# One encoder layer on one core: products with V all in every second step, a copy on ScalarE, expert ordering in pieces, sixteen unread products

## The reference

```
u = rmsnorm(x); z = u @ w_in      # q-latent, kv-latent, rotary key, two LRU branches
att = softmax((qn @ kn + qp @ kp) * scale) @ v      # 8 heads, 128 queries at a time
lru = bidirectional RG-LRU * gelu(gate)
x = x + concat(rmsnorm(att), rmsnorm(lru)) @ w_out
t = rmsnorm(x)
g = argmax(t @ w_group + b)                          # one of 4 groups
top 2 of the 8 experts of group g, softmax weights * group weight
for e in 32 experts:
    out += gate[:, e] * ((silu(t @ w_gate[e]) * (t @ w_up[e])) @ w_down[e])
y = rmsnorm(x + out)
```

## Time and profile before

| | us |
|---|---|
| median of 3 runs | 710.38 (709.85 to 711.94) |
| profiled execution | 709.74 |
| span of its profile, first to last instruction | 707.9 |
| busy in it: PE / DVE / ACT / POOL | 663.6 / 390.4 / 259.1 / 235.2 |
| moved by DMA | 155.85 MB, 220 GB/s mean |
| mean granted TensorE clock | 0.978 of full |

### The profile page before, as it was taken

The page is one execution under the profiler, slowest core; times in us unless marked ns, Lnnn a source line. Parts: engine busy times, 40 slices in busy tenths (PEclk is TensorE's granted clock), DMA queues, the critical chain, the costliest instruction groups (busy, mean ns, idle before and its releaser), DMA issues.

```text
span 707.9 us, 12135 instructions
## 1 busy us (share of the span) xinstructions
PE 663.6 (94%) x4288; PEld 443.9 (63%) x4288; DVE 390.4 (55%) x914; ACT 259.1 (37%) x482; POOL 235.2 (33%) x295
## 2 busy tenths in 40 slices
PE   3899999999999999999998659999999999999984
PEld 3887887886546666588887645566555555555531
DVE  3673589553975666637888686852323233232327
ACT  5624787733666767722111201111111111111123
POOL 5244254101925559920000131245232322323110
PEclk9999999999999999999999569999999999999999
DMA  7912210020061000063422899999999999999767
GB/s 230 260 46 52 60 33 28 20 107 31 0 234 64 1 2 2 2 237 122 147 90 76 340 384 416 418 413 409 417 415 415 416 416 416 416 415 416 291 250 301
DMA packets 50914, 155.85 MB, mean 220 GB/s; under 512 B 9509, under 2 KB 22949, under 8 KB 42673
## 3 DMA queue, kind: packets, MB, share of 16 engines
q1 hardware_dynamic: 42704, 136.32, 49.8%
q0 software_dynamic: 6432, 12.60, 4.7%
q10 hardware_dynamic: 1728, 6.29, 2.4%
HBM read 169.86 MB, written 19.92 MB: 268 GB/s over the span
## 4 chain that ended last, share of the span: by engine, by line
PE 85%; DVE 7%; DMA 3%; issue 1%; ACT 1%; POOL 1%; SPq 0%; POOLq 0%; DVEq 0%; ACTq 0%
PE bank L1031 17%; PE bank L768 16%; PE bank L1058 10%; PE bank L949 9%; PE bank L806 6%; PE bank L1005 3%; PE bank L789 3%; PE bank L838 3%; PE bank L815 3%; PE bank L723 2%; PE bank L901 2%; PE bank L1044 2%; PE bank L793 1%; PE bank L797 1%; PE bank L830 1%
## 5 line engine op out<-in xcount | busy, mean ns | idle before, releaser
L1031 PE MATMUL bank<-ring,tmp 128*64 128x256 f32 x896 | 100.6, 383 | 3.7 <-issue 3.6
L647 POOL DMA_INDIRECT expert_rows<-mix,row_now x40 | 40.0, 1000 | 161.8 <-ACT mix L1331 146.8
L1031 PEld LDWEIGHTS bank<-ring,tmp 128*64 128x64 f32 x896 | 65.5, 139 | 40.8 <-issue 11.6
L768 PE MATMUL bank<-u_high,w_high 128*128 128x256 f32 (+3 forms) x224 | 77.9, 348 | 4.3 <-DVE u_low L1585 3.0
L768 PE MATMUL bank<-u_high,w_low 128*128 128x256 f32 (+3 forms) x224 | 76.0, 339 | 0.0
L768 PE MATMUL bank<-u_low,w_high 128*128 128x256 f32 (+3 forms) x224 | 75.9, 339 | 0.0
L1324 ACT ACTIVATE rope<-bank 64x256 f32<-64x256 f32 x40 | 15.1, 378 | 144.3 <-PE bank L1031 132.2
L949 PE MATMUL bank<-ring_parts,mix_parts 128*128 128x512 f32 x240 | 64.8, 397 | 0.0
L637 POOL DMA_INDIRECT tmp<-xn_rows,idx_now x22 | 23.1, 1049 | 115.2 <-DMA xn_rows<-tmp 97.9
L1860 DVE SCALAR_TENSOR_TENSOR rope<-rope,bank 64x256 f32<-64x256 f32 x40 | 16.6, 415 | 79.2 <-ACT rope L1324 78.4
L1331 ACT ACTIVATE mix<-bank,gate_now 128x512 f32<-128x512 f32 x40 | 27.5, 687 | 88.0 <-PE bank L1058 88.0
(11 more groups left out here) (317 smaller groups left out, 1222.6 us busy)
## 6 DMA issues: line engine op xcount, KB each, us to landing
ring<-in_w_up SPq DMA_DIRECT2D x28, 1024.0 KB
ring<-in_w_down SPq DMA_DIRECT2D x28, 1024.0 KB
ring<-in_w_gate SPq DMA_DIRECT2D x28, 1024.0 KB
mix<-in_w_gate SPq DMA_DIRECT2D x12, 1024.0 KB, 10.8
mix<-in_w_up SPq DMA_DIRECT2D x12, 1024.0 KB, 13.9
mix<-in_w_down SPq DMA_DIRECT2D x12, 1024.0 KB, 15.1
ring<-in_w_in SPq DMA_DIRECT2D x13, 512.0 KB, 4.2
ring<-expert_rows SPq DMA_DIRECT2D x12, 512.0 KB, 8.5
```

The lines of the kernel that those rows point to most:

```text
L647: po.indirect_dma_start(ys_d.rearrange("r (t n) -> (r t) n", t=2), bass.IndirectOffsetOnAxis(row_now[:, 2 * j + q:2 * j + q + 1], 0), ysb[ ...
L768: last = pe.matmul(psum[u % ZB][0:m, 0:tn], w[:, t % W_RING, k, 0:m], x[:, k, t0:t0 + tn], start=(k == 0 and p == 0), stop=(k == DC - 1 an ...
L1031: last = pe.matmul(psum[q][t * WB:(t + 1) * WB, 0:F], xT[:, j, c, q * WB:(q + 1) * WB], w[:, (t * DC + c) * F:(t * DC + c + 1) * F], start ...
```

## The change

Four edits.

1. **V products.** `values(m, part)` becomes `values(m)`: all products of a pair stand in the even step, none in the odd one. The waits for the copied probabilities (`pTe`) and, for pair 1, for the branch sums (`lrs`) now stand ahead of the `rb` products instead of between them and the V products.
2. **First copies on ScalarE.** The two copies of the first experts' transposed rows go from VectorE (`rows_out(0, 0, 0)` and `(0, 0, 1)`, behind `pack_near`) to ScalarE, which is waiting there.
3. **Expert ordering in pieces.** `order_far` is cut in two (`order_far`, 13 small operations, and `order_steps`, 3 large ones), and these, the 20 `put_expert` calls and `codes_in` are put between the steps of the first four pairs' `pair_silu`, instead of ahead of and between whole pairs. `expert_codes` on TensorE goes from pair 2 to pair 3.
4. **Unread products in the gap.** `idle_work(n)` issues n products of the identity with 384 columns into a bank that nobody reads; 3, 3, 4 and 6 of them are put into the gap. Two waits for `tt` are added ahead of the first two, so that the bank is free. On GpSimd the wait for `idx` goes behind five others.

```diff
-            po.wait_ge(g("idx"), 2)
             po.wait_ge(g("xnst0"), 8 * NT)
...
             po.wait_ge(g("x2st1"), 8 * NT)
+            po.wait_ge(g("idx"), 2)
...
-            def values(m, part):
+            def values(m):
...
+                pe.wait_ge(g("pTe"), 2 * m + 2)
+                for t in range(2):
...
+                last.then_inc(g("rb"), 1)
+                for b in range(blocks):
...
-                if n >= 2:
-                    values((n - 2) // 2, n % 2)
+                if n >= 2 and n % 2 == 0:
+                    values((n - 2) // 2)
...
+            def idle_work(n):
+
+                for _ in range(n):
+                    pe.matmul(psum[7][:, 0:3 * P], ident, consts[:, CONSTS["ident"]:CONSTS["ident"] + 3 * P],
+                              start=True, stop=True)
+            pe.wait_ge(g("tt"), 2 * NT - 2)
+            idle_work(3)
             turn_rows2(NT - 1)
             router(NT - 1)
+            pe.wait_ge(g("tt"), 2 * NT)
             pe.wait_ge(g("x2"), 2 * NT)
             rows_near(0, 2 * NT - 2)
+            idle_work(3)
             ranks(NT - 1)
             rows_near(2 * NT - 2, 2 * NT)
             totals()
+            idle_work(4)
             pe.wait_ge(g("spread"), 1)
...
+            idle_work(6)
             pe.wait_ge(g("xg0"), 16)
...
-            pair_products(0, 2, expert_codes)
-            pair_products(1, 0)
+            pair_products(0, 2)
+            pair_products(1, 0, expert_codes)
...
+            for half in range(2):
+                ac.wait_ge(g("xgp"), half + 3)
+                ac.activation(xT[:, 0, 4 * half:4 * half + 4, :], psum[2 + half][:, :].rearrange("p (c n) -> p c n", c=4),
+                              ACT.Copy).then_inc(g("xT"), 1)
...
             pack_near(v, link)
-            rows_out(0, 0, 0)
-            rows_out(0, 0, 1)
             spread_rows_in(v, link, 0)
-            order_far(v, link)
...
-            pair_silu(0, 0)
+            pair_silu(0, 0, lambda: order_far(v, link))
+            order_steps(v, link)
             tables_out(v, link, 0)
...
+            put_far(0, 5)
+            pair_silu(0, 1, lambda: put_far(5, 9))
+            put_far(9, 12)
+            gates_out(v, 0)
+            put_far(12, 16)
+            pair_silu(0, 2, lambda: put_far(16, NFAR))
             far_firsts(v, link)
             jobs_in(v, link)
-            gates_out(v, 0)
-            pair_silu(0, 2, lambda: codes_in(v, link))
             rounds_in(v, link)
             spread_rows_in(v, link, 1)
-            pair_silu(1, 0)
+            pair_silu(1, 0, lambda: codes_in(v, link))
```

39 lines of the change are left out of this document (16 added, 23 removed).

## The result

The changed kernel takes **707.69 us** (median of 10 runs, 706.24 to 709.59) against 710.65 for the kernel before (10 runs, 709.68 to 714.18): a ratio of 0.9954, with a 95% interval of 0.9941 to 0.9967. The profiled execution took 707.46, with a span of 705.6; the one of before took 709.74. The forecast was 707.0, with 704.0 to 710.0 as its range. Several of its markers were wrong all the same.

The account below looks back on a forecast made before the run. TensorE bounds the kernel ahead of the weight stream; at the last pair weights and TensorE arrive together. 709.74 - 3.2 (attention) - 0 (the rest) = 706.5, given as a median of 707.0, range 704.0 to 710.0.

Parts of the forecast that it names:

- Attention: Attention stage: fewer switches between whole array and halves save 5.4 us, new waits cost 2.2; net gain 3.2 us.
- the largest at the last pair: Attention, ahead of `rb` (L832): idle in few rows, the largest at the last pair, where 0.76 us is no longer hidden.
- The start of the stream, all 3.2 of it: Behind attention: GpSimd causes no wait and the output product runs as before, so all 3.2 us reach the weight stream's start.
- TensorE is about 7 us ahead by pair 3: First expert pairs: ScalarE's copies and ordering in pieces, with attention's gain, put TensorE about 7 us ahead by pair 3.
- No idle of PE until about pair 17: Expert pairs: sign in the changed trace that TensorE has no idle time until about pair 17.
- Worth 0: Copies and ordering edits: TensorE's lead becomes waits for weights at pairs 18 and 19; 0 us, bounds -0.5 to +0.8.
- Rival A: Experts: TensorE is the bound after all, so the 7 us count too; 699.5 us, or between; 12%.
- 20 us of loads are queued: First expert pairs: codes reach SyncE one pair later, but 20 us of queued loads cover that.
- The granted clock 1.00 through the gap: Gap between output stage and first experts: sign in the changed trace that PE's clock stays at 1.00.
- Holes at pairs 18 and 19: Last expert pairs: holes of 1 to 3 us ahead of L1039, ended by DMA.
- Rival C: Pairs 18 and 19: the clock falls in the new waits for weights; 708 to 710 us; 10%.
- Rivals B and D: Attention: B, it gains little, 708.7 by the sum, 15%; D, `rb` late in every pair, 713 to 714, 5%.

Follow-up runs that it names:

- e1_values: The kernel before with only the V products of a pair put together in the even step; 706.75 us, ratio 0.9939.
- e7_best: The changed kernel without unread products, far experts' codes between pair 3's two experts, `rows_low` in halves; 704.68 us, ratio 0.9926.
- e2_rest: The changed kernel with only the V products put back in two halves; 712.16 us, ratio 1.0023.
- e4_noidle: The changed kernel without the sixteen unread products; 705.52 us, ratio 0.9926.
- e9_before_late: The kernel before, with down-weight loads from pair 6 on bringing only half of each row; 710.11 us, ratio 0.9994.
- e10_rest_late: The changed kernel with V products in two halves again and down-weight loads halved from pair 6 on; 709.01 us, ratio 0.9978.
- e3_order: The changed kernel with expert ordering and codes back where they were before; 706.01 us, ratio 0.9926.
- e6_rest_light: The changed kernel with V products in two halves again and gate and up loads halved for pairs 3 to 5; 708.41 us, ratio 0.9965.

## Why the prediction came out as it did

**Attention: right in its mechanism, and its number by luck.** Forecast 3.2 us, measured 3.22 over the stage in the changed kernel, but 4.10 in e1_values with the same edit: one wait of 0.94 decides. And two errors cancel. The waits ahead of `rb` sum to 3.9 us where the kernel before has 0.25, so 3.65 more, forecast at 2.2. The shorter products gave 6.9, forecast at 5.4. From start to start over the whole stage, the V products gave 3.2 (2.3 was the forecast: a long pair takes 0.97 to 1.00 instead of 1.03, and short pairs save 0.14 each as well), the scores 2.1 (2.3; only 22 odd steps have scores), the transposes 1.25 and `rb` 0.3 (0.8 was taken for these and the short pairs). The last pair's 0.76 was right (0.78), the pair before it 0.46 for 0.4. Where VectorE makes a row of the low part, 0.25 was counted once, and it was 1.15 and 0.94; e7_best, with the rows in halves, took both away. What failed there: VectorE's row took 2.68 us in the trace of before at its longest (270.11, L1763), and this was not weighed against the 1.4 us that VectorE has free in a pair (an estimate: it is busy for 33.35 of the 50 us from 250 to 300, and a pair takes 4.2). So "the largest at the last pair" was wrong too.

**The start of the stream, all 3.2 of it: right.** It moves from 387.08 to 383.50, by attention's 3.22 and the 0.37 from ahead of it, and e1_values alone reaches 0.9939. GpSimd delayed nothing: first output product to first load takes 83.6 us in both.

**"TensorE is about 7 us ahead by pair 3": right for the mechanism, wrong for the changed kernel.** e2_rest has 6.7 there. The changed kernel should have had attention's 3.2 on top and has 6.0 in all (453.78 against 459.77). The unread products at the lower clock cost the difference: e4_noidle, without them, has 8.7 (451.07). By pair 5 the changed kernel's lead is 4.4 (484.32 against 488.68), for the codes have moved into pair 3 with a wait of 1.30 us on VectorE at 462.44. "No idle of PE until about pair 17" was wrong, by that wait and one of 1.45 at 421.02.

**"Worth 0", since weights and TensorE arrive together: right.** It rested on one estimated landing, 661 to 662, and the semaphore shows 661.3. That the lead is lost to the weights was measured by e9_before_late and e10_rest_late: 4.4 us of it reach pair 19 only when the weights are out of the way. Rival A falls.

**"20 us of loads are queued" behind the late codes: wrong, and the step that failed most.** The one depth that the prediction had read is the 22.2 us of pair 17. At pair 3 it was 10 to 12 us: the last two loads are issued at 451.39 and 454.12, the DMA share falls from about 464, and the first of the two has landed at 465.75. The codes held SyncE until 465.93. "TensorE is half a pair ahead" is no help: a lead counts there only by as much as it is more than the stream's own, and the stream started 3.6 us earlier while pair 3 came 6.0 earlier. The last weights land 2.1 us earlier than before (659.2) instead of 3.6. That covers the 0.8 us between the forecast start of pair 19, 658.6, and the 659.38 seen, and so most of the 0.96 between the sum, 706.5, and 707.46. The loss belongs to the profiled execution, where the unread products ran at the lower clock; whether the others have it is not known.

**"The granted clock 1.00 through the gap", "the first gate and up product 6 us earlier": both wrong in the profiled execution.** The clock was 0.50 from 390.70 to 404.35, and the product 3.62 us earlier. The mean clocks of the others say that the fall was shorter in most of them. The text did price that case (the six ahead of the rows end 3 us late); the marker took only the other. The price of 0 for the stream left out that a later pair 3 makes the codes later. It lies within what was measured, though e4_noidle leans to a loss.

**Holes at pairs 18 and 19: half right.** There is one hole, of 1.91 us, at pair 19, and none at 18.

**The marker on the DMA share in 401 to 412** was to show the prediction wrong if the share rose, and it rose, from 0.75 to 0.94. It was no test: a stream that starts 3.6 us earlier raises it by itself.

**Rival C** got 10%. It did not occur in the profiled execution of the changed kernel, but it is real: e4_noidle's shows the clock fall behind a wait of 2.03 us at pair 19, and e7_best's in one of 2.63 on VectorE at pair 3. Rivals B and D did not occur: there is no wait in the ordinary pair beyond 0.12.

## What to carry to other kernels

When two resources arrive together at the end, ask for each edit which of the two it moves: e10_rest_late's 4.4 us of TensorE's lead were worth nothing until the weights were lighter, while of the 4.2 us by which e1_values starts its stream earlier 3.9 were left at the last landing. A step that feeds the engine that issues loads must be timed against the depth of the queue in microseconds at that place, and not at another place or against the lead of the engine that computes. Two edits, neither of which empties a queue alone, can empty it together. Taking a long instruction's cover away (here half of a V product) makes every other long instruction on the helping engine a candidate for a wait: list them all, and cut them to the size of the free time.

## What was not expected of the hardware

Near-full work did not raise the granted clock at once: TensorE was 93% busy from 392 to 404 with unread products and stood at 0.50, while in e2_rest the same products came with a fall of 3.4 us only (394.5 to 397.9). In the five profiled kernels with unread products the fall in the gap lasted 13.7 us (the changed kernel), 6.8 (e3_order, e6_rest_light) and 3.4 (e2_rest, e10_rest_late), in the nine without them 23.9 to 30.7. The Trainium skill (TensorE: Matmul & The Clock Gate, What's actually happening) has the clock follow how busy the engine has been. These five agree with it on the whole; the 12 us of the changed kernel do not.

One form of instruction varied more than twofold in time. A row of the low part, 128x1024 on VectorE with two inputs from SBUF, took 1.28 us at 258.87 in the changed kernel and 3.23 at 265.76, where GpSimd ran a subtraction of 128x1024 from 265.56 to 267.91; and GpSimd's cast of 128x128 behind it took 1.28 us, 0.29 elsewhere. In e7_best half a row took 0.74, and 2.31 where GpSimd's same subtraction ran. At 281 to 285 a row and GpSimd's instruction of 128x1024 at L584 started together: the changed kernel has 2.15 and 2.84 us for the two, e1_values 1.27 and 3.91. So either engine can be the one that is held up. The Trainium skill (GPSIMD Engine Reference, Specifications) names this case, VectorE with two SBUF inputs contending with GpSimd. The rows agree with it, though no run here moved the one away from the other on purpose.

A change between products on the whole array and on its two halves comes with about 0.1 us each time, on either side of it: the same scores take 0.96 behind V products and 0.86 behind transposes, the same transposes 0.53 ahead of V products or `rb` and 0.44 ahead of scores.
